# Prompt attention of a FoX and dilated-window layer: dilated sets regrouped by residue, 25 score tiles a head in place of 37

## What is computed

```python
# FoX: causal, with a bias from the cumulated log forget gates
s = einsum(q, k) / 8 + c[query] - c[key];  o_fox = softmax(causal(s)) @ v
# dilated sets: (window, dilation) = (128, 1), (512, 4), (2048, 16)
to_res = lambda t: t.reshape(B, L, dilation, H, D).transpose(0, 2, 1, 3, 4)
o, lse = band_attn(to_res(q), to_res(k), to_res(v), window // dilation)   # for each set
a = softmax(lses);  o_dil = sum over sets of a * o
```

## Time and profile before

| | us |
|---|---|
| median of 3 runs | 1780.08 (1778.94 to 1781.48) |
| span of the profiled execution | 1779.2 |
| PE busy, whole span | 1710.8 (96%) |
| DVE, ACT, POOL busy | 1086.7, 956.5, 868.4 |
| last sample work to first product of `finish` | 1068.75 to 1255.98 |

### The profile page before, as it was taken

One profiled execution on the slowest core, in us unless ns is written; L12 is line 12 of the kernel. 1 busy time (PEld: TensorE's weight loads), 2 busy tenths in 40 slices (PEclk: granted clock), 3 DMA queues, 4 the chain that ended last, 5 costly groups with the idle time before them and its releaser, 6 DMA issues. The chain is left out here.

```text
span 1779.2 us, 32332 instructions
## 1 busy us (share of the span) xinstructions
PE 1710.8 (96%) x10749; PEld 1529.3 (86%) x10749; DVE 1086.7 (61%) x2480; ACT 956.5 (54%) x1649; POOL 868.4 (49%) x496
## 2 busy tenths in 40 slices
PE   6999999999889999999999977898999999999998
PEld 5888888899889999899899956888998989899897
DVE  6747556422388888888888877888444514234251
ACT  5444344432368887888888877988314313122230
POOL 1615233300338878778788747775233433333332
PEclk9999999999999999999999998999999999999999
DMA  7386585645889999999999976320645566666662
GB/s 238 106 290 216 202 300 183 207 132 137 253 308 365 344 351 350 353 347 336 355 360 349 316 232 163 91 73 25 215 146 214 235 259 236 259 236 260 236 259 77
DMA packets 191563, 427.76 MB, mean 240 GB/s; under 512 B 22761, under 2 KB 86122, under 8 KB 190002
## 3 DMA queue, kind: packets, MB, share of 16 engines
q1 hardware_dynamic: 187474, 415.29, 66.8%
q10 hardware_dynamic: 2560, 8.39, 1.6%
q0 software_dynamic: 1376, 2.10, 0.5%
HBM read 392.36 MB, written 120.64 MB: 288 GB/s over the span
## 5 line engine op out<-in xcount | busy, mean ns | idle before, releaser
L1086 POOL TENSOR_TENSOR vv_lo<-v_raw,vv_hi 128x1024 fp32r<-128x1024 f32 x178 | 401.4, 2261 | 147.9 <-ACT vv_hi L1175 145.7
L1986 POOL TENSOR_TENSOR w_lo<-w_raw,w_hi 128x2048 fp32r<-128x2048 f32 x39 | 180.1, 4619 | 318.4 <-ACT w_hi L2000 318.4
L1167 ACT ACTIVATE kt_hi<-ktp 128x1024 fp32r<-128x1024 f32 (+1 forms) x192 | 186.2, 970 | 94.0 <-PE ktp L1351 93.2
L1191 DVE TENSOR_TENSOR kt_lo<-ktp,kt_hi 128x1024 fp32r<-128x1024 f32 (+1 forms) x192 | 220.9, 1151 | 8.1 <-ACT kt_hi L1167 6.2
L1365 PE MATMUL s_ps<-kt_hi,q_st 128*128 128x256 f32 (+3 forms) x768 | 205.9, 302 | 0.8 <-DVE mx_parts L1241 0.4
L1351 PE MATMUL ktp<-ident,k_raw 128*128 128x128 f32 x1440 | 192.0, 276 | 8.3 <-DVEq L1182 3.8
L1351 PEld LDWEIGHTS ktp<-ident,k_raw 128*128 128x128 f32 x1440 | 168.6, 142 | 32.7 <-issue 5.6
L707 PE MATMUL acc<-w_hi,xn_hi 128*128 128x512 f32 x480 | 192.4, 401 | 2.4 <-POOL w_lo L340 2.4
L1175 ACT ACTIVATE vv_hi<-v_raw 128x1024 fp32r<-128x1024 f32 (+1 forms) x192 | 191.4, 997 | 6.2 <-PE o_ps L1381 5.7
L1365 PE MATMUL s_ps<-kt_lo,q_st 128*128 128x256 f32 (+3 forms) x768 | 191.0, 282 | 0.0
L707 PE MATMUL acc<-w_lo,xn_hi 128*128 128x512 f32 x480 | 187.7, 391 | 0.0
(11 more groups left out here) (244 smaller groups left out, 4139.4 us busy)
## 6 DMA issues: line engine op xcount, KB each, us to landing
k_raw<-in_cache_fox_k SPq DMA_DIRECT2D x256, 256.0 KB, 4.9
v_raw<-in_cache_fox_v SPq DMA_DIRECT2D x256, 256.0 KB, 4.6
out_win_kv_sample<-in_cache_win_kv SPq DMA_DIRECT2D x32, 2040.0 KB, 9.5
w_raw<-in_w_in SPq DMA_DIRECT2D x32, 1024.0 KB, 5.9
k_raw<-in_cache_win_kv SPq DMA_DIRECT2D x40, 512.0 KB, 9.5
v_raw<-in_cache_win_kv SPq DMA_DIRECT2D x40, 512.0 KB, 8.6
w_raw<-in_w_up SPq DMA_DIRECT2D x16, 1024.0 KB, 5.3
w_raw<-in_w_down SPq DMA_DIRECT2D x16, 1024.0 KB, 5.1
```

Of the source, the lines that this page charges most:

```text
L1086: gp.tensor_tensor(vv_lo[:, slot, 0:tiles, :], v_raw[:, i % RAW_RING, 0:tiles, :], vv_hi[:, slot, 0:tiles, :].bitcast(F32), ALU.subtract). ...
L1167: act.activation(kt_hi[:, slot, :, 0:n], ktp[:, i % 2, :, 0:n], ACT.Copy).then_inc(k_hi, 1)
L1191: ve.tensor_tensor(kt_lo[:, slot, :, 0:n], ktp[:, i % 2, :, 0:n], kt_hi[:, slot, :, 0:n].bitcast(F32), ALU.subtract).then_inc(k_lo, 1)
L1986: gp.tensor_tensor(w_lo[slot][:], w_raw[:, slot, :], w_hi[slot][:].bitcast(F32), ALU.subtract).then_inc(slab_lo_done, 1)
```

## The change

1. **Tiles.** The sets of dilation 4 and 16 are kept in scratch ordered by residue mod 4 (ACT writes the turned queries and keys with a rearranged pattern; the values are loaded with one). 512 tokens are 4 residues of 128, so each of these sets needs only 4 tiles of 128 x 128 a head, 8 together, called SPREAD; the set of dilation 1 is NEAR (7 tiles), FoX is FAR (10 tiles).
2. **Steps.** A head has 7 steps (`GROUPS`): two SPREAD, two NEAR, three FAR, each of 3 or 4 tiles. 56 steps in all.
3. **Shares.** Probabilities are no longer divided. Each kind keeps its minimum of negated scores and its sum of exponentials per query. SPREAD statistics are by residue, so the NEAR ones go through DRAM (`stat_s`) to that order; DVE, POOL and ACT compute each kind's share; shares go through DRAM (`share_s`) to all partitions; POOL `scale` multiplies the outputs with them, one pair at a time.
4. **Inputs piece by piece.** A pair's queries and keys are split in 12 pieces: hi by DVE (queries) and ACT (keys), all 12 lo by POOL. The first pair's pieces are made in the last steps of `attend_sample`, where DVE also clears the zero halves of the queries, and SP loads queries and keys one step after the last group, ahead of the last value loads.
5. **Stores.** Turned queries and keys are stored once in four tiles in place of each tile; the bias is stored as 10 tiles a head.

```diff
+GROUPS = ((SPREAD, (0, 1)), (SPREAD, (2, 3)), (NEAR, (2, 3)), (NEAR, (0, 1)), (FAR, (3,)), (FAR, (2,)), (FAR, (0, 1)))
+S_BANKS, T_BANKS, STATS = 3, 2, 3
+KEEP_BEHIND, EXP_P_BEHIND, TURN_BEHIND, LOW_BEHIND = 1, 2, 4, 5
+SPREAD_BEHIND, NEAR_BEHIND, FAR_BEHIND = (6, 7, 9), (10, 11), (12, 13)
+PIECE_STEP = (0, 1, 2, 2, 3, 3, 4, 5, 5, 6, 7, 7)
+PIECES_BEFORE = ((5, 8, 11), (6, 9, 12))
+PIECES_BEHIND, FIRST_PIECES_BEHIND = 8, 6
+def piece_lo(gp, ahead, p, j):
...
+    gp.tensor_tensor(part_of(ahead, p, 1, hh, s), raw_cols(ahead, hh, s), part_of(ahead, p, 0, hh, s).bitcast(F32), ALU.subtract).then_inc(ahead["part_lo"], 1)
# attend_sample
-            straight(DEC_BATCH, PER_BATCH, (0, load_keys), (0, load_first_values), (EXP_BEHIND, load_values))
-            sp.wait_ge(parts_lo, 2)
-            load_query_half(sp, a, qk_raw, pair_in, 0, 0)
-            load_pair_keys(sp, a, qk_raw, pair_in, 0)
-            load_query_half(sp, a, qk_raw, pair_in, 0, 1)
+            straight(DEC_BATCH, PER_BATCH, (0, load_keys), (0, load_first_values), (EXP_BEHIND, load_values), (1, first_pair), (4, first_masks))
...
+            def clear_queries(hh):
+                def stage(b, i):
+                    if b == DEC_BATCH - 1 and i == LAST:
+                        done(ve, s_done, group_index(b, LAST))
+                        ve.memset(ahead["q"][64 - 64 * hh:128 - 64 * hh, :, hh].bitcast(F32), 0.0).then_inc(ahead["zeroed"], 1)
+                return 4 + hh, stage
# attend_prompt, SP
+                    sp.wait_ge(exp_done, STEPS * h + 4)
+                    sp.dma_start(a["stat_s"][h].rearrange("c (q p) -> p (c q)", p=P), stat[:, h % STATS, NEAR].rearrange("p c q -> p (c q)"), allow_slow_non_contiguous=True).then_inc(near_sent, 16)
...
+                    sp.dma_start(near_stat[:, h % STATS], a["stat_s"][h].rearrange("c (m r) -> m c r", r=RESIDUES)).then_inc(near_in, 16)
...
+            straight(HEADS, STEPS, (3, raw_queries_ahead), (3, raw_keys_ahead), (6, values_ahead), (6, send_near), (7, take_near), (8, bias_ahead),
+                     (10, send_far), (17, send_shares), (18, take_shares))
# POOL
+            def scale(h, i):
+                if i or h % 2 == 0:
+                    return
...
+                gp.tensor_tensor(x, x, share[:, 2, :], ALU.mult)
+                gp.wait_ge(copied[NEAR], h + 1)
+                gp.tensor_tensor(near, near, share[:, 1, :], ALU.mult).then_inc(scaled_apart, 1)
+                gp.wait_ge(scaled_apart, p + 1)
+                gp.tensor_tensor(near, near, x, ALU.add)
+                gp.wait_ge(copied[FAR], h + 1)
+                gp.tensor_tensor(far, far, share[:, 0, :], ALU.mult).then_inc(scaled, 1)
+            straight(HEADS, STEPS, (0, mask_diagonals), *(pieces_lo(j) for j in range(len(PIECES))),
+                     *(values_lo(w, first) for w in range(SETS) for first in (True, False)), (14, gaps), (15, weights), (16, divide), (20, scale))
# ACT
+                for n in units:
+                    x, (least_of, sum_of) = probs[:, prob_cols(i, n)], (stat[:, h % STATS, kind, c, n:n + 1] for c in range(2))
+                    last = act.activation(x, x, ACT.Exp, scale=-1.0, bias=least_of, accum_out=sum_of)
# DVE
+                        ve.tensor_copy(part_of(ahead, p, 0, hh, s), raw_cols(ahead, hh, s)).then_inc(q_hi, 1)
# PE
+                    if kind == SPREAD:
+                        lots = [(s, slice(n * P, (n + 1) * P), slice(cols.start + j * P, cols.start + (j + 1) * P)) for j, (s, _) in enumerate(unit_tiles(kind, n))]
...
+                    for s, keys, out in lots:
+                        for m, (mine, theirs) in enumerate(((0, 0), (1, 0), (0, 1))):
+                            last = pe.matmul(s_ps[:, at % S_BANKS, out], q[:, mine, h % 2, s, n * P:(n + 1) * P], k[p % 2][:, theirs, s, keys], start=(m == 0), stop=(m == 2))
# project_tokens, ACT
+                    act.activation(token_cols(y_cols, t, by_residue), turned_cols(tp[:, slot, :], by_residue), ACT.Copy).then_inc(yt_done, 1)
```

More of the change, by code:

```diff
@@ L1399 @@
[L1399 to L1425, removed]
+SPREAD, NEAR, FAR = 0, 1, 2
@@ new lines, in turns_hi @@
+            def turns_hi(h, i):
+                kind = GROUPS[i][0]
+                jobs = len((SPREAD_JOBS, NEAR_JOBS, FAR_JOBS)[kind])
+                after(act, weighed[kind], jobs * h - (1 if kind == SPREAD and i == 0 else 0))
+                act.wait_ge(turned, STEPS * h + i + 1)
+                for cols, places in turned_parts(i):
+                    last = act.activation(pt_hi[:, places, :], t_ps[:, (STEPS * h + i) % T_BANKS, cols].rearrange("p (k n) -> p k n", n=P), ACT.Copy)
+                last.then_inc(turned_hi, 1)
@@ L1827, in turn @@
+            def turn(h, i):
+                at = STEPS * h + i
+                pe.wait_ge(exp_done, at + 1)
+                after(pe, turned_lo, at - T_BANKS + 1)
                 hold(pe)
-                for n in range(len(tiles_of(i))):
-                    last = pe.transpose(t_ps[:, i % BANKS, n * P:(n + 1) * P], probs[:, s_at[qt, s] + n * P:s_at[qt, s] + (n + 1) * P], ident[:])
+                first = prob_cols(i, GROUPS[i][1][0]).start
+                for n in range(group_cols(i) // P):
+                    last = pe.transpose(t_ps[:, at % T_BANKS, n * P:(n + 1) * P], probs[:, first + n * P:first + (n + 1) * P], ident[:])
@@ new lines, in weigh_far, with key_rows @@
+            def weigh_far(job):
+                def key_rows(h, i):
+                    if i:
+                        return
+                    p = h // 2
+                    pe.wait_ge(v_lo_done, SETS * p + 4)
+                    pe.wait_ge(turned_lo, STEPS * (h + 1))
+                    if job == 0:
+                        after(pe, copied[FAR], h)
+                    hold(pe)
+                    for kt in FAR_JOBS[job]:
+                        count, first = Q_TILES - kt, FIRST_SLOT[FAR] + 4 * kt
+                        for m, (v, x) in enumerate(((v_hi, pt_hi), (v_lo, pt_hi), (v_hi, pt_lo))):
+                            last = pe.matmul(o_ps[:, FAR, kt * P:SEQ], v[:, v_slot(p, 3), kt, :], x[:, first:first + count, :],
+                                             start=(kt == 0 and m == 0), stop=(kt == Q_TILES - 1 and m == 2))
+                    last.then_inc(weighed[FAR], 1)
+                return FAR_BEHIND[job], key_rows
@@ L1861 @@
+            straight(HEADS, STEPS, (0, score), (TURN_BEHIND, turn), *(weigh_spread(job) for job in range(len(SPREAD_JOBS))),
+                     *(weigh_near(job) for job in range(len(NEAR_JOBS))), *(weigh_far(job) for job in range(len(FAR_JOBS))))
 LEFT_ROOM = 4 * (2 * 2 + 2) * N_TOK
```

800 lines of the change are left out of this document (432 added, 368 removed).

## The result

The changed kernel takes 1846.82 us in the median of 4 runs (1841.77 to 1851.22), the kernel before 1780.78 (1778.94 to 1783.22) beside it: ratio 1.037, 95% interval 1.0346 to 1.0394. That is 66 us slower, and far outside the predicted range. The profiled execution, the fastest of the four, has a span of 1840.0.

The account below looks back on a forecast made before the run. PE work bounds the kernel (busy 96%). Stage 2.4 + 131 + 2 + 22 = 157.4, plus 12 and 1: 170.4 against 186.9; gain 16.5, less 2, 14.5; span 1779.2 to 1764.7, median 1766, range 1745 to 1790.

Parts of the forecast that it names:

- Part 3: End of the stage, last score to `finish`: 22, range 17 to 30; sending 4-byte NEAR statistics 3.5, upper bound 8.
- Edits costed at nothing: Stores, bias stores, ACT copies and SP's `part_lo` waits cost nothing; shares held up to two steps, `scale` late enough.
- Part 1: Tiles: PE work 14.6 a head, 29.2 a pair, 117 where 146 stood; taken at 1.2 times, 35 a pair.
- Part 2: Head of the stage: first scores start 2.4 after the last sample work; lower clock costs about 2.
- Part 4: Tail of the sample stage ends 12 later, bounds 3 and 20; two DVE clears 3.6 each, added pieces and loads.
- B: Rival: POOL and DVE block one another; a pair takes 43, 30 more, 1796; decides from 39 a pair; chance 0.16.
- C: Rival: tail of the sample stage takes all 20, end exchange 27; 13 more, 1779, no difference; chance 0.1.
- A: Rival: rings and idle time absorb the sample tail (3 for 12), a pair takes 32; 20 less, 1746; chance 0.2.
- D: Rival: tiles fall but chain latency with 2 turned banks holds the period; 35 becomes 38, 1777; chance 0.08.

Follow-up runs that it names:

- e12: Changed kernel with statistics and FAR shares 8 bytes apart in SBUF, same number of 4-byte pieces, each partition writing neighbouring DRAM addresses: 1837.07 us, ratio 1.0315.
- e1: Changed kernel with both scattering sends in runs of 16 bytes, reordering by residue left out: 1787.77 us, ratio 1.004.
- e5: Changed kernel with 16-byte runs in both scattering sends and take_near, take_shares, scale at stages 11, 22, 27; reordering by residue left out: 1778.67 us, ratio 0.9993.
- e3: Changed kernel with take_near at stage 11 for 7, take_shares 22 for 18, scale 27 for 20; 4-byte sends unchanged: 1822.65 us, ratio 1.0241.
- e4: Changed kernel with the two DVE clears in the sample tail cut into 16 of 512 elements, one a step: 1841.47 us, ratio 1.0347.
- e6: e4 with SP loading masks and bias at stage 12 in place of 4 in the sample tail: 1844.98 us, ratio 1.0374.
- e11: e9 with the last six of the first pair's twelve pieces split in steps 0 to 3 of the prompt's stage: 1770.37 us, ratio 0.9944.
- e7: Complete changed kernel, PE transposing statistics and FAR sums for sends in 512-byte runs, stages as in e3 but sends at 9 and 12: 1780.55 us, ratio 1.0002.
- e9: e7 with 16 small clears in place of 2 and masks and bias loaded at stage 12: 1775.04 us, ratio 0.9968.
- e8: e3 with both 4-byte scattering sends issued from ACT's queue in place of SP's: 1823.75 us, ratio 1.0237.

## Why the prediction was wrong, step by step

The forecast stage, put on the time axis: sample end 1081.1, first score 1083.5, last score 1218.5, `finish` 1240.5. The changed kernel has 1088.4, 1089.6, 1272.4, 1318.6. So the tail is 7.3 too late, the way to the first score 1.2 shorter, the scores 47.8 longer and the end 24.2 longer, 78.1 in sum; `finish` took 2.8 less than forecast, which leaves the 75.3 between the spans 1764.7 and 1840.0. The median of the runs lies 6.8 above the profiled span here, so against 1766 the miss is 81.

- **Part 3, the price of the 4-byte send, failed.** It was taken as 3.5, with 8 as the bound; landing took 9.7 in the median of e12, and a wait of SP for one in the changed kernel 8.5 to 12.7. The nearest row, 2 KB in 2.0 us, was of longer pieces and said nothing of a transfer of 1024 pieces. I chose the value nearer to it against the count of pieces, which stood in the same sentence.
- **"Edits costed at nothing" failed, and it is where the price of the send did its harm.** The step said that SP's waits hold the shares back by up to two steps and that `scale` comes late enough. I looked at one wait (`part_lo`) and not at the take behind each send: four round trips a pair, all in SP's one list, were never summed. Even at my own upper bound of 8 they would have been some 32 us a pair; at 10 to 12 they are 46, and `scale`, with five pieces behind it, closed the ring. How the two share the loss, e1 and e5 tell: from first to last score the changed kernel takes 182.8, e1 146.8, e5 133.7. So with sends that land in 4.0, near the 3.5 assumed, the waits would still have cost 13 of these 49 us; the other 36 need the waits and the long sends together. In the time of the kernel e1 gives 59 us, e3 24, both in e5 68.
- **Part 1, the tiles, right.** In e5 the scores take 133.7 from first to last, forecast 135 (131 + 2 + 2), and a pair 36.3, forecast 35. POOL has 30 a pair, as counted. The 128-column products are 0.11 apart as before. The forecast had taken this from the rows and not the 56 ns of the Trainium skill (TensorE: Matmul & The Clock Gate, the 56 ns gap), and that was right.
- **Part 2, the head, right:** 1.2 us against 2.4.
- **Part 4, the tail, too small:** 19.3 against 12, inside its bounds. The clears were right to 0.1 (3.47 each). Not in the sum: SP's masks and bias, which wait for the last score with value loads behind them (3.2 us, e4 to e6). POOL's pieces were understated: half of them are worth 4.7 net of what they cost in the stage (e11).
- **Part 3, the end, without the slow sends:** 29.7 in e5 and 30 in e7, where the range of 17 to 30 ended. In the trace of e7 four scalings of 1.26 follow shares that land at 1249.7, and ACT's `left_hi` of 3.2 us stands ahead of the small exponential. That last one was not foreseen.
- **Rivals.** B (1796): the outcome was on its side, its mechanism was not. DVE's copies of query pieces in the changed kernel take 0.42 us in the median of 24, with 1.38 the longest, and e5's pair of 36.3 lies under its point of decision, 39. Its evidence had also been misread. The split of line L1743 was long not once but three times, 2.03, 1.81 and 1.80, once in each pair but the first, and the POOL operation beside it was the normalisation of 2.3 us, not one of 1.3. Each time the split ended 0.55 us after that operation, as here:

```profile
1157.83 2.31 POOL L1619 TENSOR_TENSOR probs<-probs,r_den 128x1280 f32<-128x1280 f32 x1
1158.89 1.80 DVE L1743 TENSOR_TENSOR q_lo<-qk_raw,q_hi 64x512 fp32r<-64x512 f32 x1
```

So POOL did hold such a split of two operands back; the copies that replaced it were hardly held. The rule of port locking in the Trainium skill (SBUF — State Buffer, Who interferes with whom) may be behind single rows of the tail too, as this one of DVE (the shortest 512-column split of this line takes 0.68; POOL has back to back operations until 1064.92, 0.6 us before this one ends), but no run here tests it alone:

```profile
1061.57 3.96 DVE L1328 TENSOR_TENSOR vv_lo<-v_raw,vv_hi 128x512 fp32r<-128x512 f32 x1
```

C (tail 20, end 27, 1779) is what the change does with its sends mended: e7 has 1780.55. But the changed kernel itself, which C was about, did not come near it. A and D didn't come about: the tail was not absorbed, and a pair is not 38.

No rival had the slow exchange as a ring through SP. It should have been one: the prediction's own rows, two sends without a row of their kind and an engine with one list, named its place.

## What to carry to other kernels

Look at the pieces of a transfer, how many and how small, and not only at its bytes. Price a small exchange through DRAM as send plus wait plus take, times how often one queue goes through it in a period; compare that sum with the period. If a wait stands in a list, write down what is behind it, and follow whether that is what the wait itself depends on a turn later. And to measure an edit beside a ring of waits, break the ring first: e6 showed nothing, e9 showed the same edits at 5.5 us.

## What the runs showed of the hardware that was not expected

A send of 4 KB in 1024 pieces of 4 bytes took 9.7 us to land in the median (e12), in 256 pieces of 16 bytes 4.0 (e1); in 8 runs of 512 bytes the take followed 2.9 us after the send (e7). 512 pieces of 4 bytes were no shorter, 10.4 in the median (e12). Most of the time passes after the last recorded packet: 8.5 us at the end of the changed kernel, where e1 has about 1. In such a gap a large load on another queue ran at 0 to 35 GB/s but for one slice, where it reached over 400 behind it, and issuing the send from another queue gained nothing (e8 against e3). Neighbouring DRAM addresses written from different partitions are not what costs (e12). A DVE split with two operands in SBUF that began beside a POOL operation of 2.3 us took 1.80 to 2.03 us in place of 0.69, three times in the kernel before.
